# Context tiles placed among the stick-breaking attention steps of a two-block transformer kernel, and memory attention run by halves

## What is computed

```python
# first block, layer 0: gated short convolution; layer 1: stick-breaking attention
for i in range(2):
    h = rmsnorm(x, mix_norm[i])
    mem_k, mem_v = mem_n @ w_mem_kv[i]                      # 4 heads of 64
    if i == 0:  y_main = b_gate * causal_short_conv(c_gate * u, conv_w)
    else:       y_main = stick_breaking_attention(q, k_sh, v_sh)     # 12 heads of 64
    y_mem = softmax(q_mem @ mem_k.T) @ mem_v                # memory attention
    x = x + concat(y_main, y_mem) @ w_o[i]
    x = x + swiglu(rmsnorm(x, ffn_norm[i]))
x = rmsnorm(x, final_norm)
# stick breaking, per head
z = q @ k.T / 8;  log_not = where(causal, log_sigmoid(-z), 0)
a = where(causal, exp(log_sigmoid(z) + reverse_cumsum(log_not) - log_not), 0);  out = a @ v
# second block: its context (256 tokens of its own) gives the start states
sh, sc, ... = silu(c) @ w_ada + b_ada                       # for c and for c_ctx
hc = rmsnorm(ctx) * g * (1 + sc) + sh
k, v, lr = hc @ w_in[:, OFF_KVG:];  s_f, s_b = states(k, v, log_decay(lr))
hx = modulate(rmsnorm(x)); ... gated linear attention, spatial gating, convolutional ffn
```

## Time and profile before

| | |
|---|---|
| median of 3 runs | 1209.74 us |
| the profiled execution | 1211.49 us, span 1210.2 us |
| mean granted TensorE clock | 0.984 |
| TensorE busy (matmul) | 96% of the span, 9014 matmuls |
| VectorE, ScalarE, GpSimd busy | 69%, 51%, 12% |
| HBM read | 219.42 MB, 182 GB/s over the span |

### The profile page before, as it was taken

One profiled execution on the slowest core, in us unless ns is written; L12 is line 12 of the kernel. 1 busy time (PEld: TensorE's weight loads), 2 busy tenths in 40 slices (PEclk: granted clock), 3 DMA queues, 4 the chain that ended last, 5 costly groups with the idle time before them and its releaser, 6 DMA issues.

```text
span 1210.2 us, 21837 instructions
## 1 busy us (share of the span) xinstructions
PE 1157.9 (96%) x9014; PEld 1110.4 (92%) x9014; DVE 833.1 (69%) x1278; ACT 622.6 (51%) x938; POOL 149.4 (12%) x111
## 2 busy tenths in 40 slices
PE   7999999999899899999999999999999989999996
PEld 6999999999788789999998898979899988999995
DVE  5677677778774756877787756577646767677775
ACT  5655444445564645444455664656437444555553
POOL 0003000000100012000000000000001032344431
PEclk9999999999999989999999999999999997999999
DMA  8655587776744144877877445354324552556550
GB/s 310 195 163 178 165 295 253 240 246 229 244 128 136 51 157 146 263 263 252 274 265 232 160 157 166 105 174 140 114 95 158 185 182 90 186 178 192 175 157 36
DMA packets 60467, 221.90 MB, mean 183 GB/s; under 512 B 6752, under 2 KB 7008, under 8 KB 59984
## 3 DMA queue, kind: packets, MB, share of 16 engines
q1 hardware_dynamic: 59904, 219.06, 55.0%
q10 hardware_dynamic: 288, 1.05, 0.2%
q0 software_dynamic: 176, 0.39, 0.1%
HBM read 219.42 MB, written 1.05 MB: 182 GB/s over the span
## 4 chain that ended last, share of the span: by engine, by line
PE 81%; DVE 10%; ACT 5%; issue 3%; DMA 1%; SPq 0%; POOL 0%; ACTq 0%; DVEq 0%
PE PS L350 23%; PE PS L352 22%; PE PS L351 22%; PE PS L355 13%; DVE w_lo L1316 4%; ACT w_hi L837 3%; DVE PS L1889 1%; DVE SQ L1587 1%; DMA ARENA<-memT 1%; DVE raw L1338 0%; DVE SQ L1352 0%; DVE ARENA L1352 0%; PE PS L455 0%; DVE H_lo L1362 0%; ACT ARENA L925 0%
## 5 line engine op out<-in xcount | busy, mean ns | idle before, releaser
L1316 DVE TENSOR_TENSOR w_lo<-raw,w_hi 128x1024 fp32r<-128x1024 f32 x325 | 398.8, 1228 | 259.9 <-ACT w_hi L837 259.4
L837 ACT ACTIVATE w_hi<-raw 128x1024 fp32r<-128x1024 f32 x356 | 372.5, 1054 | 141.7 <-PE PS L352 117.4
L350 PE MATMUL PS<-Y_hi,w_hi 128*128 128x256 f32 x1240 | 358.4, 289 | 9.6 <-DVE w_lo L1316 4.2
L351 PE MATMUL PS<-Y_lo,w_hi 128*128 128x256 f32 x1240 | 353.9, 285 | 0.0
L352 PE MATMUL PS<-Y_hi,w_lo 128*128 128x256 f32 x1240 | 353.8, 285 | 0.0
L350 PEld LDWEIGHTS PS<-Y_hi,w_hi 128*128 128x128 f32 x1240 | 240.8, 194 | 16.2 <-issue 9.4
L351 PEld LDWEIGHTS PS<-Y_lo,w_hi 128*128 128x128 f32 x1240 | 241.2, 194 | 0.4 <-issue 0.2
L352 PEld LDWEIGHTS PS<-Y_hi,w_lo 128*128 128x128 f32 x1240 | 241.0, 194 | 0.0
L350 PE MATMUL PS<-H_hi,w_hi 128*128 128x256 f32 x808 | 232.1, 287 | 5.3 <-DVE w_lo L1316 2.8
L351 PE MATMUL PS<-H_lo,w_hi 128*128 128x256 f32 x808 | 229.3, 284 | 0.0
L352 PE MATMUL PS<-H_hi,w_lo 128*128 128x256 f32 x808 | 229.2, 284 | 0.0
(11 more groups left out here) (206 smaller groups left out, 1316.7 us busy)
## 6 DMA issues: line engine op xcount, KB each, us to landing
raw<-stream SPq DMA_DIRECT2D x404, 512.0 KB, 4.2
ARENA<-memT SPq DMA_DIRECT2D x2, 512.0 KB, 7.7
X<-xT SPq DMA_DIRECT2D x1, 1024.0 KB, 11.4
ARENA<-c_rows SPq DMA_DIRECT2D x2, 512.0 KB, 8.2
ARENA<-memT SPq DMA_DIRECT2D x1, 1024.0 KB, 7.1
ARENA<-ctxT SPq DMA_DIRECT2D x1, 1024.0 KB, 8.1
outT<-ARENA SPq DMA_DIRECT2D x2, 512.0 KB, 2.6
CROW<-c_rows SPq DMA_DIRECT2D x1, 512.0 KB, 10.2
```

Source lines behind the costliest of these rows:

```text
L350: pe.matmul(o, wh, xh, start=start, stop=False, skip_group_check=True)
L351: pe.matmul(o, wh, xl, start=False, stop=False, skip_group_check=True)
L837: act.activation(w_hi[n % RING][:], raw[at][:], ACT.Copy).then_inc(*mark("hi", n))
L1316: dve.tensor_tensor(w_lo[n % RING][:], raw[raw_of("slot", n)][:], w_hi[n % RING][:], ALU.subtract).then_inc(*mark("lo_dve", n))
```

## The change

- Three of the 13 context slots move ahead of `w_o1`: `ctx_lr` and two of `ctx_k` stand behind `kv_v1`, before `side.finish()`. The other ten stay behind `ffn1`.
- The context's norm moves from `ffn1` into the end of `ffn0`, its sum of squares from `w_o1` into `a_b`; its input is loaded during `a_c`. The normed context has tiles of its own (`CX`), which share the place of `CTX` and its squares.
- `memory_attention` works by halves (two heads) with steps given by `pace`, the memory attention of layer 1 starts at the first step of `b_q` beside the kv norm, and the stick-breaking groups start five steps sooner on TensorE, at the same step on all engines.
- The outputs of the stick attention are made by heads four at a time at steps 14, 16, 18 behind the first group's start, in banks 2 to 4. `w_o1` takes its eight inputs in the order 0, 1, 2, 3, 6, 7, 4, 5.
- The 16 mods that need both rows are all taken in `ffn0`, one per iteration up to the 16th; the other 32 in `ffn1`, two in every second iteration from the fourth on. The second silu of c_ctx and its load are gone.
- `block1_end` gets other steps, and `ctx_k1` uses banks 0 and 1 only.

```diff
-          ("kv_v1", 2), ("w_o1", KC), ("ffn1", FFN_SLOTS),
-          ("ctx_lr", 1), ("ctx_k", 4), ("ctx_v0", 4), ("ctx_v1", 4),
+          ("kv_v1", 2), ("ctx_lr", 1), ("ctx_k0", 2), ("w_o1", KC), ("ffn1", FFN_SLOTS),
+          ("ctx_k1", 2), ("ctx_v0", 4), ("ctx_v1", 4),
...
-    if _j % 2 == 0 and _both < CTX_MODS:
-        _now = [_both]
+    if _l == 0:
+        _now = [_j] if _j < CTX_MODS else []
     else:
-        _now = [CTX_MODS + _one + i for i in range(2 if _l and _j in (11, 13, 15, 17) else 1)]
+        _now = [len(MOD_ORDER) + _i for _i in range(2 if _j % 2 and _j > 2 else 1)]
...
+def both(first, second):
+    live = [first, second]
+    while live:
+        live = [task for task in live if next(task, "end") != "end"]
+        if live:
+            yield
...
             # TensorE, memory_attention(l)
-                yield from nothing(6)
-                pe.wait_ge(*past("ma_prob", l, 7))
-                claim(*bs)
                 for h in range(MEMH):
+                    if h % 2 == 0:
+                        yield from pace.to(7 + l + h // 2)
+                    pe.wait_ge(*past("ma_prob", l, 2 * h + 1))
+                    claim(bs[h])
...
             # TensorE, stick_outputs()
                 for c in range(MC):
-                    b = 4 + c // 2
+                    b = 2 + c // 2
                     if c % 2 == 0:
+                        yield from pace.to(14 + c)
                         claim(b)
+                    if c == 0:
+                        pe.wait_ge(*past("vs", 1))
                     pe.wait_ge(*past("am", c))
...
             # TensorE, block1_end()
+                pace = Pace()
+                yield
                 yield
                 quarters("final")
-                yield
-                yield
+                yield from pace.to(5)
                 sum_quarters("final")
-                yield
-                yield from nothing(5)
+                yield from pace.to(9)
                 quarters("norm1")
-                yield
-                yield
+                yield from pace.to(11)
                 sum_quarters("norm1")
...
             # TensorE, the second mixer
-            side = Side(nothing(KC + 1))
-            project("b_qm", 2, H, lambda i: ("qm", 1, i), side, [norm_low("mix1", k) for k in range(KC)], 2)
+            project("b_qm", 2, H, lambda i: ("qm", 1, i), None, [norm_low("mix1", k) for k in range(KC)])
             kept = 0
-            side.tasks[:0] = [nothing(1)]
-            side.tasks += [memory_attention(1), stick_schedule(stick_group, lambda: kept)]
+            side = Side(memory_attention(1), both(stick_schedule(stick_group, lambda: kept), stick_outputs()))
...
             project_tokens("kv_v1", 256, Y, (2, 3), ("vs", 1), side)
+            project("ctx_lr", 1, CX, lambda i: ("lr", 0), side, [norm_low("ctx", k) for k in range(KC)])
+            project("ctx_k0", 2, CX, lambda i: ("kb", 0, i), side)
             side.finish()
-            pe.wait_ge(*past("vs", 1))
-            stick_output()
-            side = Side(context_rms())
-            project("w_o1", KC, H, lambda i: ("added", 1, i), side, y_ready)
-            side.finish()
-            ffn(1, Side(nothing(KC + 1)))
+            project("w_o1", KC, H, lambda i: ("added", 1, i), None, y_ready, order=(0, 1, 2, 3, 6, 7, 4, 5))
+            ffn(1)
...
             # ScalarE and VectorE, the second mixer
-            side.tasks[:0] = [nothing(1)]
-            side.tasks += [memory_attention(1), stick_schedule(stick_group, lambda: kept)]
+            side.tasks = [both(memory_attention(1), chain(*side.tasks)),
+                          both(stick_schedule(stick_group, lambda: kept), stick_outputs())]
...
             # VectorE, block1_end()
-                yield from nothing(3)
+                yield
+                yield from pace.to(6)
                 dve.wait_ge(*past("rs", "final"))
                 for c in range(KC):
                     ...
-                    if c % 2:
-                        yield
-                yield from nothing(3)
+                    if c == 3:
+                        yield from pace.to(7)
+                yield from pace.to(12)
                 dve.wait_ge(*past("x_final", KC - 1))
                 yield from norms("norm1", X, ...)
...
-            ffn(0, Side(memory_norm()))
+            ffn(0, Side(memory_norm(), context_norm()))
-            ffn(1, Side(context_norm()))
+            ffn(1)
```

More of the change, by code:

```diff
@@ L1 @@
 from contextlib import ExitStack
+from itertools import chain
 import numpy as np
@@ L52 @@
 for _l, _j in ((_l, _j) for _l in range(2) for _j in range(FC)):
-    _both = sum(a < CTX_MODS for a in MOD_ORDER)
-    _one = len(MOD_ORDER) - _both
-    if _j % 2 == 0 and _both < CTX_MODS:
-        _now = [_both]
+    if _l == 0:
+        _now = [_j] if _j < CTX_MODS else []
     else:
-        _now = [CTX_MODS + _one + i for i in range(2 if _l and _j in (11, 13, 15, 17) else 1)]
+        _now = [len(MOD_ORDER) + _i for _i in range(2 if _j % 2 and _j > 2 else 1)]
     MOD_ORDER += _now
     MODS_AFTER[AT[f"ffn{_l}"] + (RING + 1 + 2 * _j if _j < 2 else RING + 3 * _j)] = _now
-assert sorted(MOD_ORDER) == list(range(NMOD))
-CTX_FFN1 = next(a for a in MODS_AFTER[AT["ffn1"] + RING + 1])
+assert MOD_ORDER == list(range(NMOD))
 LOADS = []
@@ L278, in build @@
         RS_COLS = small[:, 32:34]
-        RS_AT = {"mem0": 1, "mix0": 0, "mix1": 0, "ctx": 1, "final": 0, "norm1": 1, "out": 0}
+        RS_OF = {"mem0": RS[:, 1], "mix0": RS[:, 0], "mix1": RS[:, 0], "ctx": LR[:, 1], "final": RS[:, 0],
+                 "norm1": RS[:, 1], "out": RS[:, 0]}
         def gain(name, c):
@@ L359, in slot, with tall @@
                 return n % RING
-            def tall(o, h, ready=None, within=None):
+            def tall(o, h, ready=None, within=None, order=range(KC)):
                 nonlocal n
                 r = slot()
-                for k in range(KC):
+                for k in order:
                     if ready:
@@ L369, in tall @@
                     w = slice(k * P, (k + 1) * P)
-                    last = mm3(o, w_hi[r][:, w], w_lo[r][:, w], h[0][:, k], h[1][:, k], k == 0, k == KC - 1)
+                    last = mm3(o, w_hi[r][:, w], w_lo[r][:, w], h[0][:, k], h[1][:, k], k == order[0], k == order[-1])
                 last.then_inc(*mark("used", n))
@@ L387, in wide, with project @@
                 n += 1
-            def project(stage, count, h, release, side=None, ready=None, steps=1):
+            def project(stage, count, h, release, side=None, ready=None, steps=1, order=range(KC)):
                 assert n == AT[stage], (stage, n)
@@ L393, in project @@
                     claim(b)
-                    tall(PS[:, b, 0:T], h, ready if i == 0 else None)
+                    tall(PS[:, b, 0:T], h, ready if i == 0 else None, order=order)
                     emptied[b] = [release(i)]
@@ L458, in memory_attention @@
                     emptied[bs[h]] = [("ma_pt", l, h)]
-                    if h % 2:
-                        yield
-                claim(*os)
                 for h in range(MEMH):
+                    if h % 2 == 0:
+                        yield from pace.to(9 + l + h // 2)
+                    if h == 0:
+                        claim(*os)
                     pe.wait_ge(*past("ma_pt", l, h))
@@ L470, in memory_attention @@
                         emptied[os[c]] = [("ma_lo", l, c)]
-                        yield
-                yield
+                yield from pace.to(12 + l)
             def gate_up(l, j, ready=None, side=None, within=None):
@@ L507, in ffn @@
                 for j in range(2, FC):
-                    beside = tail if j >= FC - 4 else None
+                    beside = tail if j >= FC - 6 else None
                     gate_up(l, j, side=beside)
@@ L919, in memory_attention @@
                 nmx, sm = small[:, 8:16], small[:, 16:24]
-                yield
-                act.wait_ge(*past("ma_max", l))
+                pace = Pace()
                 for h in range(MEMH):
+                    if h == 0:
+                        yield from pace.to(2)
+                    if h % 2 == 0:
+                        act.wait_ge(*past("ma_max", l, h // 2))
                     for t in range(TT):
@@ L1223, in act_program @@
             act.dma_start(WS, sgu_wT).then_inc(*mark("late_in", 1, by=16))
-            side = Side(context_rms())
-            project("w_o1", KC, left, side, then=residual_square(1, H2, lambda c: gain("ffn1", c)))
-            side.finish()
+            project("w_o1", KC, left, then=residual_square(1, H2, lambda c: gain("ffn1", c)))
             inverse_rms("res1")
             act.preload_act_table(ACT.Silu)
-            ffn(1, Side(norm_his("ctx", Y2, lambda c: SH1(c, 1), CSQ)))
+            ffn(1)
             exp_set()
```

192 lines of the change are left out of this document (95 added, 97 removed).

## The result

The changed kernel takes 1222.39 us (median of 4 runs, 1221.18 to 1224.54), the kernel before beside it 1210.32: ratio 1.0102, 95% interval 1.0079 to 1.0126. It is 1% slower, where the forecast was 1213.9 and its range ended at 1219. In the traces TensorE's granted clock has two levels, 2.4 GHz (1.00 in the rows) and 1.2 GHz (0.50), called half clock here.

The account below looks back on a forecast made before the run. TensorE, busy 1157.9 of 1210.2 us, was taken to bound the kernel by its work plus its gaps. Terms summed to +4.2 us: 1215.7 profiled, 1213.9 as a median, range 1203.5 to 1219.

Parts of the forecast that it names:

- (c): Block end: norm chain finishes late, so `lr` waits 2.9 us, plus 0.9 for half clock behind it.
- (a): Block end: `ctx_v0` claims bank 1 straight after ctx_k1 filled it and waits for the copy, +0.6 us.
- (b): Block end: final scaling makes squares of the result end 2.0 us after TensorE wants them, +1.0 us.
- both terms: Second mixer: memory attention of layer 1, -2.8 us, and the stick groups with the tail, +3.9 us.
- the stick groups: Second mixer: log_not wanted one slot later instead of two; tails and first z products wait, together 10.2 us.
- -2.8: Second mixer: memory attention of layer 1 by halves falls from 5.7 us to 2.65 plus 0.2 for half clock.
- The rival in which they cover the tails: Second mixer: log_not ready when TensorE asks, stick stage costs 8.7 us instead of 17.6, total 1205.0; chance 0.26.
- Squares, ffn0, ffn1: Context squares +0.5 us; ffn0 start +0.5 and end -1.4; ffn1 -1.7 for its waits and -0.2 at its end.
- the half clock did repeat: Rival: second mixer's tails waits bring three more half-clock stretches from the second group on, +5.1 us, 1219.0; chance 0.10.
- once waits reach some 2.0: Second mixer: the waits, in us, at which the rival of repeated half clock was said to decide.
- Block end early enough: Rival: block end's norms cost only the bank wait and late squares, -3.8 us, total 1210.1; chance 0.17.
- the page's clock: Rival: only a wholly idle stretch lowers TensorE's clock, so no short wait costs any; total 1212.4; chance 0.05.

Follow-up runs that it names:

- c_all: Changed kernel with group tails one step later, block end's norms two half-slots earlier, ctx_k1 in banks 2 and 3, context squares' products and outputs one step later: 1200.64 us.
- the lag put back: Changed kernel with TensorE's second-mixer memory attention ending one step later than on ScalarE and VectorE, as in the kernel before: 1204.85 us, ratio 0.9951.

## Why the prediction was wrong

The sign was the forecast's and the size was not: +4.2 summed, +10.5 measured.

**The step that failed** is the last part of the block end's (c), "half clock behind it, one chance in two: 0.9". It measured 5.5. The waits themselves were near (2.9 laid out, 2.4 measured); what I priced was one stretch of 1.7 us, and there were three full of work (half of 10.3 us is 5.1; the other 0.4 is not separated). I had not looked at what TensorE runs directly behind the waits in `lr`: the sixteen-row products. With all rows in them one stretch was left, and with the norms in time `lr` and `k` took 7.2 us less. The price of a fall depends on the instructions behind it. The rest of the error is in smaller terms: 1.0 each in the context slots and in the mixer, 1.1 net in places that had no term, less 0.5 each in the waits of `lr`, in ffn1 and ahead of `a_u`.

**Block end (a) and (b)**: +1.6 against +2.6 for the ten slots, a little too small; the experiment that moved both gave 0.8 back.

**Second mixer**: both terms held in their gaps (12.9 us of waits and 5.3 for the outputs laid out, 11.6 and 4.4 measured). The prediction named the cause too ("with all engines starting at one step" TensorE wants log_not one slot later "where before it had two"), and then booked it under the stick groups while it gave memory attention by halves its -2.8. Counted by edit instead of by place, halving as written cost 5.6 us (1222.39 against 1216.82), and with one yield more the same kernel takes 1204.85, 12.0 us less than with memory attention whole. The sum is not hurt by such booking, but the reading was: I took for a price of the change what was a slip of one step in it.

**The tiles**: "the three slots themselves hide what they can" was right in the changed kernel. The rival in which they cover the tails (1205.0) failed on the 5.1 us of chain, as argued against it. With the lag back the tails are covered as it has them.

**Squares, ffn0, ffn1**: within 0.5 us each. For the squares the net (+0.5, +0.7) is right by luck, with two errors that cancel: `a_b` got 3.1 us longer, 1.5 of it because TensorE goes at ScalarE's pace there (run c_all), and `w_o1` 2.4 shorter.

**Rivals**: the half clock did repeat, but not in the mixer where I looked for it (1219.0): the tails' waits of 1.2 to 1.4 us every 9.8 us had none behind them. Its "once waits reach some 2.0" does not hold either: the clock fell behind waits of 1.10 and 1.31 us, and not behind the 2.47 of the last tails. "Block end early enough" fell. So did "the page's clock", the rival by the rule of the Trainium skill that the prediction cites: half clock came at 705 behind a stretch with 1.24 of 3.40 us of work.

**Not foreseen**: stretches at 807 and 872 behind waits that both kernels have. The changed kernel around 807, and the kernel before around the same wait, each cut in step with its own trace's half-clock stretches:

```profile
804.00:807.40 3.40, 0.87 (x9) 0.87 (x9) 3.40 (x4) 3.40 (x6) 0.00 (x0) 1.00 0.45 154
807.40:810.80 3.40, 3.40 (x11) 2.73 (x9) 3.40 (x4) 0.69 (x1) 0.00 (x0) 0.50 0.48 154
```

```profile
792.21:795.62 3.41, 2.40 (x11) 1.67 (x9) 3.41 (x5) 1.85 (x2) 0.00 (x0) 1.00 0.48 154
795.62:799.04 3.42, 1.86 (x12) 1.69 (x13) 3.42 (x4) 3.12 (x5) 0.00 (x0) 1.00 0.51 153
```

The wait is 2.57 us in both, and only one of them pays 1.6 us behind it. In the changed kernel it lies whole in one stretch; in the kernel before it is divided between two. The sixteen traces go the same way at this place: in ten most of the wait lies in one stretch and the clock falls (the changed kernel among them, and later tails alone), in six it is divided more evenly and the clock stays (the kernel before, tiles behind ffn1, later tails with the block end earlier). At 872 it is the same, in five traces against eleven. No edit was made near either place; what differs is the time at which the wait comes, which edits ahead of it move. The two places are worth up to 3 us either way in any comparison here, and that part is luck.

## What to carry to other kernels

When generators of several engines are rewritten together, count their yields: a difference of one step between TensorE and its producers can be a schedule's slack, and losing it turned every group into a wait. Before pricing a late input, read what runs behind the wait: a fall of the clock ahead of sixteen-row products cost three stretches at half clock, ahead of the same products over all rows one. Whether a wait of some 2.5 us brings a fall at all changed with where it lay, and an edit far ahead of it can move that; compare such kernels by stages. Filler slots moved into a stage that waits for its own order bring nothing until that order is mended; mend first, then see whether cover is still wanted.

## What the runs showed of the hardware

Half clock behind waits of 1.10 and 1.31 us lasted 10.3 us with sixteen-row products behind them and 3.4 with the same products over all 128 rows; in both cases the fall came ahead of these products. It rose again behind the first stretch without sixteen-row products: the third, the second (memory attention whole) and the first. That rests on one trace with full rows; the three stretches came in three traces (the changed kernel, later tails, the lag put back). The same sixteen-row products without a wait ahead ran at full clock in the kernel before (1.99 us for eight). A wait of 2.57 us brought half clock where it lay in one stretch (0.87 us of work) and none where it was divided (2.40 and 1.86).

The Trainium skill (TensorE: Matmul & The Clock Gate, Part 1, table of the two states) has the half rate come after an idle window; the trace has such a case ahead of `w_o1`, and at 705 the clock fell without one.

```profile
441.90:445.60 3.70, 0.00 (x0) 0.00 (x0) 2.31 (x6) 1.82 (x3) 0.00 (x0) 1.00 0.40 142
445.60:449.00 3.40, 3.09 (x15) 2.40 (x16) 1.55 (x4) 0.60 (x1) 0.00 (x0) 0.50 0.08 17
```

Accumulating matmuls whose inputs arrive one by one show no gap between them, only a longer group (2.10 against 1.07 us for sixteen): a wait can hide inside busy time.
